# Output projection by seven products in place of eight, in an encoder step of two mixers

## The chip, the cores and the metric

The kernel runs on one core of a Trainium2 chip. The metric is the device time in microseconds (us) of one execution, launch to end; lower is better. TensorE (PE in the rows) multiplies matrices, VectorE (DVE), ScalarE (ACT) and GpSimd (POOL) work element by element, and SyncE (SP) issues nearly all DMAs. Each engine takes its instructions in program order and waits on semaphores.

## The reference, cut to what matters

```python
xn = rms_norm(x, norm_g)                      # x: 512 prompt rows and 32 sample rows, 1024 features
h  = xn @ w_in                                # one projection; its columns feed everything below
oa = sparse_attention(...)                    # top-k keys per query, 8 heads of 64
ob = stick_breaking_attention(...)            # 8 heads of 64
ya = (oa * silu(ua)) @ w_a_out                # 512 -> 1024
yb = (ob * silu(ub)) @ w_b_out                # 512 -> 1024
mixed = sigmoid(ga) * ya + sigmoid(gb) * yb
y  = x + mixed @ w_o                          # 1024 -> 1024, the product that is changed
```

All arrays are float32. The new rows of keys and values are outputs too.

## The kernel before, in words

Prompt and sample tokens lie side by side as 544 columns (`NT`), features on the partitions, in 8 chunks of 128 (`KC`). Most products take two halves of 272 columns (`HALF_NT`), one PSUM bank each. To keep float32 accuracy, each operand is split into a high part (ACT copies it to fp32r) and a low part (DVE subtracts the high part from the raw value), and a product is three matmul passes: high by high, high by low, low by high (`PASSES`).

Weights come in units of 256 columns, 1 MB each (`UNITS`). SP loads them into two raw buffers; ACT writes `whi` (`w_high`, L1051) and DVE `wlo` (`w_low`, L1452).

The changed part is the last 105 us. Its stages, in order:

1. Fast gates (L958). The last five gate features are computed by the seven-product form of a 2 by 2 block product: K in two halves, tokens in two halves. The weight sums t1 to t4 and the quarters b11, b22, b21 stand in a slot (two slots of 7 quarters of 512 columns, each with high and low part). Slot 0 lies where queries and keys were, slot 1 over `whi` and `wlo`. DVE makes the weight sums (L1963 to L1968) and takes products off PSUM with ACT.
2. Mixes (L989). For each of 8 output features d (chunks of 128), branch B's product and branch A's product, 48 matmuls of 272 columns. DVE then multiplies both with the sigmoids (L1996), adds them (L1999), ACT makes the high part (L1432) and DVE the low part (L2001) of the mixed value, and the two make the next-but-one unit's weights (`w_high`, `w_low`). Mix d has its own set of four PSUM banks, used by every other d, and waits for the weights and for d-2's banks.
3. Output projection (L1004). 16 groups (8 features, 2 halves) of 24 matmuls. Each group's result is added to a residual copy of x in `res` (L2009) and stored (L555). `out_group` runs the first three groups up to the last K chunk while the last mixed feature is being finished. `whi`/`wlo` are filled by unit, one ahead.

In the mixing stage POOL does nothing: its program ends with the additions for the last sample rows (L2072). Earlier it multiplies attention weights (L2082) and takes roots (L2094).

Of the kernel before, what the change touches and what calls it, by code (L numbers as in the profile page):

```python
# [8 lines left out]
F32 = mybir.dt.float32  # L9
F32R = mybir.dt.float32r  # L10
# [5 lines left out]
P = 128  # L16
# [178 lines left out]
def direct_index(u):  # L195

    return sum(kind != "fast" for _, kind in UNITS[:u])
# [37 lines left out]
OUT_BANK = [4, 5, 6, 7, 0, 1, 2, 3]  # L235
# [15 lines left out]
SUM_STEPS = (0, 1, 3)  # L251
FAST_BANKS = [{"a": 0, "b": 2, "c": 4}, {"a": 1, "b": 3, "c": 5}]
# [6 lines left out]
def build(nc, x_kw_qi, cache_a_k, cache_a_v, cache_idx_k, cache_b_k, cache_b_v, q_norm_g, k_norm_g,  # L259
# [3 lines left out]
    with ExitStack() as ctx:  # L263
# [16 lines left out]
        xhi = by(KC, sb("xhi", KC * NT, F32R)[:, :])  # L280
        xlo = by(KC, sb("xlo", KC * NT, F32R)[:, :])
# [90 lines left out]
        res = by(KC, sb_at("res", KC * NT, F32, at_q)[:, :])  # L372
# [13 lines left out]
        for n, c, h in (("x11", 0, 0), ("x12", 4, 0), ("s3", 0, 1), ("x22", 4, 1)):  # L386
# [5 lines left out]

        slots_hi = [sb_at(f"slot_hi{k}", SLOT, F32R, at)[:, :] for k, at in enumerate((at_q, at_whi))]
# [11 lines left out]
        const_in, cache_i_in, cache_bk_in, cache_bv_in, cache_ak_in, cache_av_in, res_in = (  # L405
            sem(n) for n in ("const_in", "cache_i_in", "cache_bk_in", "cache_bv_in", "cache_ak_in", "cache_av_in",
                             "res_in"))
# [27 lines left out]
        y_done, y_out = sem("y_done"), sem("y_out")  # L435
# [3 lines left out]
        def wview(buf, uu):  # L439

            return by(2 * EC if UNITS[uu][1] == "mix" else KC, buf[:, uu % 2, 0:unit_cols(uu)])

# [38 lines left out]
        def _(sp):  # L481
            def load_unit(name):
# [6 lines left out]
                sp.dma_start(raw[:, uu % 2, 0:unit_cols(uu)], src).then_inc(raw_ready[uu % 2], 16)  # L489
# [57 lines left out]
            for name, _ in UNITS[U["gate2"]:]:  # L547
                load_unit(name)
                if name == "mix2":
                    sp.wait_ge(f_done, len(PRODUCTS) * len(FAST))  # L550
                    sp.dma_start(res, x_kw_qi.rearrange("c p n -> p c n")[:, :, 1:FIRST_AT]).then_inc(res_in, 16)
            for g in range(2 * KC):
                e, h = divmod(g, 2)
                sp.wait_ge(y_out, g + 1)
                sp.dma_start(y_fm[:, e, halved(h)], res[:, e, halved(h)]).then_inc(st_y, 16)  # L555
# [6 lines left out]
        def _(pe):  # L562
# [409 lines left out]
            def mix(d):  # L972
# [20 lines left out]
                mm.then_inc(mix_done, 1)  # L993
# [4 lines left out]
            def out_group(g, chunks):  # L998

                e, h = divmod(g, 2)  # L1000
                uu = U[f"out{e // 2}"]
                for c in chunks:
                    for a, b in PASSES:
                        mm = pe.matmul(ps[:, OUT_BANK[g % 8], 0:HALF_NT], wview(wpart[b], uu)[:, c, P * (e % 2):P * (e % 2) + P],  # L1004
                                       mpart[a][:, c, halved(h)], start=(c + a + b == 0), stop=(c == KC - 1 and a == 1))
                return mm

            pe.wait_ge(mix_used, D // P - 1)
            pe.wait_ge(m_lo, D // P - 1)
            pe.wait_ge(w_lo, direct_index(U["out0"]) + 1)  # L1010
            for g in range(3):
                out_group(g, range(KC - 1))
            pe.wait_ge(m_lo, D // P)
            for g in range(3):
                out_group(g, [KC - 1]).then_inc(y_done, 1)
            pe.wait_ge(mix_used, D // P)
            for g in range(3, 2 * KC):
                if g % 4 == 0:
                    pe.wait_ge(w_lo, direct_index(U[f"out{g // 4}"]) + 1)
                if g >= 8:  # L1020
                    pe.wait_ge(y_out, g - 7)
                out_group(g, range(KC)).then_inc(y_done, 1)

        @block.scalar
        def _(act):
# [408 lines left out]
            for o in range(2, D // UC):  # L1434
                w_high(f"out{o}")
# [764 lines left out]
```

## Time and profile before

| | us |
|---|---|
| median of 3 runs (524.34 to 526.58) | 525.01 |
| the profiled execution, its own time | 523.65 |
| its span in the trace | 521.9 |
| PE busy in the span | 515.1 (99%) |
| DVE busy | 370.7 (71%) |
| ACT busy | 258.2 (49%) |
| POOL busy | 76.7 (15%) |
| output projection, first to last matmul | 470.7 to 519.3 |

The rows below quote lines of the trace. An instruction line begins with its start and duration in us; a bracket at its end tells how long the engine sat idle before it and what ended that.

### The profile page before, as it was taken

What the parts mean: (1) busy time and instruction counts of PE and PEld (TensorE: products, weight loads), DVE (VectorE), ACT (ScalarE), POOL (GpSimd) and SP (SyncE); (2) the same over time, 40 slices, a digit from 0 to 9 for tenths busy, and PEclk for the clock granted to TensorE, in tenths of its full rate; (3) what the DMA queues carried; (4) which work ended last, traced back from release to release, by engine and by line L of the source; (5) the groups of instructions that cost most, each with busy time, mean ns of one, the idle gap of its engine ahead of it and who ended that gap; (6) DMA issues with size and microseconds to landing.
All of it is one profiled execution on the core that took longest, in us unless ns stands there. A gap on an engine that the chain in (4) does not pass through costs nothing.

```text
span 521.9 us, 10124 instructions
## 1 busy us (share of the span) xinstructions
PE 515.1 (99%) x4188; PEld 485.5 (93%) x4188; DVE 370.7 (71%) x718; ACT 258.2 (49%) x434; POOL 76.7 (15%) x73
## 2 busy tenths in 40 slices
PE   8999999999999999999999999999999999999997
PEld 6889999999998988989998888999999999999997
DVE  5878758899979989478857668563987556665331
ACT  7655764344366566864244665653566532231100
POOL 3506000014034314284000000000000000000000
PEclk9999999999999999999999999999999999999999
DMA  7623305142331322023230016020232172245111
GB/s 274 266 80 123 92 1 167 35 168 82 117 133 28 140 82 82 1 82 122 87 113 4 1 47 212 2 82 1 82 105 98 42 252 80 82 162 189 50 52 46
DMA packets 15359, 50.45 MB, mean 97 GB/s; under 512 B 2288, under 2 KB 6000, under 8 KB 11728
## 3 DMA queue, kind: packets, MB, share of 16 engines
q1 hardware_dynamic: 15168, 49.49, 27.6%
q8 instruction: 33, 0.54, 0.4%
q10 hardware_dynamic: 144, 0.30, 0.2%
q14 instruction: 14, 0.11, 0.1%
HBM read 42.82 MB, written 6.82 MB: 95 GB/s over the span
## 4 chain that ended last, share of the span: by engine, by line
PE 91%; DVE 4%; issue 2%; ACT 2%; DMA 1%; ACTq 0%
PE PS L665 40%; PE PS L1004 9%; PE PS L958 8%; PE PS L989 8%; PE PS L619 4%; PE PS L784 3%; PE PS L765 3%; PE PS L649 3%; PE PS L869 2%; PE PS L741 2%; PE PS L710 2%; PE PS L849 1%; PE PS L690 1%; PE PS L598 1%; PE PS L793 1%
## 5 line engine op out<-in xcount | busy, mean ns | idle before, releaser
L665 PE MATMUL PS<-xhi,whi 128*128 128x272 f32 x320 | 94.6, 296 | 0.0
L665 PE MATMUL PS<-xlo,whi 128*128 128x272 f32 x320 | 92.4, 289 | 0.0
L665 PE MATMUL PS<-xhi,wlo 128*128 128x272 f32 x320 | 92.1, 288 | 0.0
L1452 DVE TENSOR_TENSOR wlo<-raw,whi 128x2048 fp32r<-128x2048 f32 (+1 forms) x31 | 64.5, 2080 | 17.3 <-ACT whi L1051 15.9
L665 PE MATMUL PS<-whi,xhi 128*128 128x256 f32 x256 | 73.4, 287 | 0.8 <-DVE nmx L1844 0.8
L665 PE MATMUL PS<-wlo,xhi 128*128 128x256 f32 x256 | 72.4, 283 | 0.0
L665 PE MATMUL PS<-whi,xlo 128*128 128x256 f32 x256 | 71.9, 281 | 0.0
L665 PEld LDWEIGHTS PS<-xhi,whi 128*128 128x128 f32 x320 | 60.3, 189 | 2.9 <-issue 2.3
L1051 ACT ACTIVATE whi<-raw 128x2048 fp32r<-128x2048 f32 (+1 forms) x31 | 52.1, 1682 | 18.2 <-PE PS L1004 18.2
L665 PEld LDWEIGHTS PS<-xhi,wlo 128*128 128x128 f32 x320 | 60.4, 189 | 0.0
L665 PEld LDWEIGHTS PS<-xlo,whi 128*128 128x128 f32 x320 | 60.2, 188 | 0.0
L665 PEld LDWEIGHTS PS<-whi,xhi 128*128 128x128 f32 x256 | 48.2, 188 | 2.4 <-issue 1.2
L665 PEld LDWEIGHTS PS<-whi,xlo 128*128 128x128 f32 x256 | 48.5, 189 | 0.0
L665 PEld LDWEIGHTS PS<-wlo,xhi 128*128 128x128 f32 x256 | 48.2, 188 | 0.0
L2082 POOL TENSOR_TENSOR wk<-wk 128x766 f32<-128x766 f32 (+2 forms) x13 | 27.8, 2140 | 70.6 <-DVE wk L1741 70.6
L1004 PE MATMUL PS<-xhi,whi 128*128 128x272 f32 x128 | 37.0, 289 | 1.1 <-DVE wlo L1452 1.1
L1004 PE MATMUL PS<-xlo,whi 128*128 128x272 f32 x128 | 37.1, 290 | 0.0
L989 PE MATMUL PS<-olo,whi 128*128 128x272 f32 x128 | 37.0, 289 | 0.0
L1004 PE MATMUL PS<-xhi,wlo 128*128 128x272 f32 x128 | 36.8, 288 | 0.0
L1741 DVE TENSOR_TENSOR_SCAN wk<-wk 128x512 f32<-128x512 f32 (+4 forms) x34 | 25.5, 797 | 12.2 <-ACT wk L1219 12.1
L2009 DVE TENSOR_TENSOR res<-res,PS 128x272 f32<-128x272 f32 x16 | 6.8, 436 | 28.0 <-PE PS L1004 28.0
L1244 ACT ACTIVATE wk<-PS 128x768 f32<-128x768 f32 (+1 forms) x24 | 21.1, 880 | 10.8 <-PE PS L765 10.8
(283 smaller groups left out, 1318.2 us busy)
## 6 DMA issues: line engine op xcount, KB each, us to landing
raw<-in_w_units SPq DMA_DIRECT2D x28, 1024.0 KB, 4.9
raw<-in_w_mixes SPq DMA_DIRECT2D x8, 512.0 KB, 3.4
stage<-in_x_kw_qi SPq DMA_DIRECT2D x7, 564.5 KB, 5.1
res<-in_x_kw_qi SPq DMA_DIRECT2D x1, 2176.0 KB, 8.1
out<-res SPq DMA_DIRECT2D x16, 136.0 KB, 1.7
out<-vals SPq DMA_DIRECT2D x2, 1024.0 KB, 6.2
out<-kT SPq DMA_DIRECT2D x1, 1088.0 KB, 8.7
out<-tm SPq DMA_DIRECT2D x1, 1024.0 KB, 8.0
```

The lines of the kernel that those rows point to most:

```text
L619: mm = pe.matmul(ps[:, t, :], xpart[a][:, c, t0:t0 + n], fpart[b][:, c, KW:FIRST], start=False, stop=(c == KC - 1 and k == 2))
L649: mm = pe.matmul(bank[0:2 * DEC, 0:UC], xst[:, c, :], wview(wpart[b], uu)[:, c, :], start=(c + b == 0), stop=(c + b == KC))
L665: mm = pe.matmul(out, lhsT, rhs, start=(k == 0), stop=(k == 23))
L765: last = pe.transpose(ps[:, 4 + r, o:o + P], pr[:, c:c + P], ident)
L958: mm = pe.matmul(ps[:, banks[b], 0:HALF_NT], weights_of(i, form, w)[:, c, :], (s_hi, s_lo)[a][block_][:, c, :], start=(opens and c + k == ...
L989: mm = pe.matmul(ps[:, MIX_BANK[d] + 2 * br + h, 0:HALF_NT], wview(wpart[b], uu)[:, EC * br + c, :], o_of(a, br, c)[:, halved(h)], start=( ...
L1004: mm = pe.matmul(ps[:, OUT_BANK[g % 8], 0:HALF_NT], wview(wpart[b], uu)[:, c, P * (e % 2):P * (e % 2) + P], mpart[a][:, c, halved(h)], sta ...
L1051: act.activation(whi[:, uu % 2, 0:n], raw[:, uu % 2, 0:n], ACT.Copy).then_inc(w_hi, 1)
L1244: last = act.activation(dst[:, :, 0:n], ps[:, 4:6, 0:n], ACT.Copy)
L1452: dve.tensor_tensor(wlo[:, uu % 2, 0:n], raw[:, uu % 2, 0:n], whi[:, uu % 2, 0:n].bitcast(F32), ALU.subtract).then_inc(w_lo, 1)
L1741: last = dve.tensor_tensor_scan(v, v, v, 1.0, ALU.mult, ALU.min)
L2082: pool.tensor_tensor(v, v, rest[:, t % 2, :, 1:n], ALU.mult).then_inc(a_done, 1)
```

## The change

The output projection gets the seven-product form too: each of four units of 256 output columns is a 2 by 2 block product (K halves, two features; K halves, two token halves). So it needs block sums of the mixed values and of the weights. K is split as chunks 0, 1, 4, 5 and 2, 3, 6, 7 (`K_HALVES`), so that a "pair" k joins one chunk of each half, and the sums s1 to s4 are made pair by pair as the mixed features come: POOL makes those of pairs 0 to 2, DVE those of the last pair. ACT and DVE split them (`sum_high_m`, `sum_low_m`). POOL makes the weight sums of all four units (`out_sums`) and the low parts of the first (`first_low`). The first unit uses slot 0, filled while the mixes run; the second uses slot 1, over `whi` and `wlo`, and so is filled after the last mix; the others follow in turn. The two mix units share one raw buffer, the other serves unit 0. The residuals are loaded in four parts into gate buffers that are used up. Each mix's branch B is multiplied with its gate as soon as it is done, branch A after; the last mix is handled by token halves. Products are added to the residual one by one (`out_added`): 8 for the first unit, 7 for each other.

```diff
+K_HALVES = ((0, 1, 4, 5), (2, 3, 6, 7))
+M_FORMS = ("s1", "s2", "s4", "s3")
+FIRST_OUT = [("p1", "b11", "x11", "a"), ("p2", "b21", "x12", "c"), ("p4", "t4", "x22", "d"), ("p5", "t1", "s1", "b"),
+             ("p6", "t2", "s2", "a"), ("p3", "b22", "s4", "b"), ("p7", "t3", "s3", "a")]
+FIRST_TAKEN = [("p1", 0, 0), ("p2", 0, 0), ("p4", 0, 1), ("p5", 1, 1), ("p6", 1, 0), ("p3", 1, 0), ("p7", 0, 1), ("p7", 1, 1)]
...
 @block.sync
+            load_out(0)
+            for name, _ in UNITS[U["mix2"]:U["out0"]]:
+                load_unit(name)
+            load_res(0)
+            load_res(1)
+            load_out(2)
+            load_out(1)
+            load_res(2)
+            load_res(3)
+            load_out(3)
...
 @block.tensor
+            def out(o):
+                for n, form, block_, b in out_products(o):
...
+                    elif n == "p6":
+                        pe.wait_ge(y_added, taken_last(o, "p1"))
+                    elif n == "p3":
+                        pe.wait_ge(y_added, taken_last(o, "p5"))
+                    elif n == "p7":
+                        pe.wait_ge(y_added, taken_last(o, "p6"))
...
+                    for c in range(KC // 2):
+                        if o == 0:
+                            if n == "p1" and c == 0:
+                                pe.wait_ge(m_lo, D // P - 1)
+                            elif n == "p2" and c == KC // 2 - 1:
+                                pe.wait_ge(m_lo, D // P)
+                            elif n == "p4" and c == KC // 2 - 1:
+                                pe.wait_ge(m_lo, D // P + 1)
+                            elif block_ in M_FORMS:
+                                pe.wait_ge(ms_low, m_form(c, block_))
+                        for k, (a, w) in enumerate(PASSES):
...
 @block.vector
-            for d in range(D // P):
-                dve.wait_ge(mix_done, d + 1)
...
+            for d in range(D // P - 1):
+                dve.wait_ge(mix_done, 3 * d + 1)
...
+                gated(d, 1, None)
+                dve.wait_ge(mix_done, 3 * d + 3)
+                gated(d, 0, None).then_inc(mix_used, 1)
...
                 dve.tensor_tensor(gates[d][:, 0, :], gates[d][:, 0, :], gates[d][:, 1, :], ALU.add).then_inc(mixed, 1)
+                m_low(d, 0, HALF_NT if d in K_HALVES[0] else NT, d + 1)
+                if d + 2 < D // P:
+                    w_low(f"mix{d + 2}")
+                if d in (4, 5):
+                    for form in M_FORMS:
+                        sum_low_m(d - 4, form)
...
+            for h in range(2):
+                dve.wait_ge(mix_done, 3 * d + 2 + h)
+                ins = gated(d, 0, h)
...
+                dve.tensor_tensor(gates[d][:, 0, halved(h)], gates[d][:, 0, halved(h)], gates[d][:, 1, halved(h)],
+                                  ALU.add).then_inc(mixed, 1)
+                if h == 0:
+                    m_low(d, 0, HALF_NT, d + 1)
+            dve.wait_ge(mixed, d + 2)
+            for form in ("s1", "s2", "s4"):
+                sum_m(form)
+            m_low(d, HALF_NT, NT, d + 2)
+            for form in M_FORMS:
+                sum_low_m(2, form)
...
+            sum_low_m(3, "s1")
+            out_added(0, 0)
+            sum_low_m(3, "s2")
+            out_added(0, 1)
+            sum_low_m(3, "s4")
+            sum_low_m(3, "s3")
+            out_added(0, 2)
+            out_low(1, 0)
+            out_added(0, 3)
...
 @block.gpsimd
+            def out_sums(o):
+                pool.wait_ge(out_raw[o % 2], 16 * (o // 2 + 1))
+                if o == 0:
+                    pool.wait_ge(f_done, len(PRODUCTS) * len(FAST))
+                elif o == 1:
+                    pool.wait_ge(mix_done, 3 * D // P)
+                else:
+                    pool.wait_ge(y_done, len(PRODUCTS) * (o - 1))
...
+                pool.tensor_tensor(both, raw_of(uu)[:, QUARTER:3 * QUARTER], raw_of(uu)[:, 0:2 * QUARTER],
+                                   ALU.subtract).then_inc(yt_done, 1)
...
+            out_sums(0)
+            for j in range(len(PARTS)):
+                first_low(j)
+            for k in range(KC // 2 - 1):
+                pair_sums(k)
+            for o in range(1, OUTS):
+                out_sums(o)
```

`out_sums` has one subtraction of 1024 columns and two of 512 that wait for one another; `first_low` four subtractions (512, then three of 1024); `pair_sums` one addition and three subtractions of 272.

## Rows read from the trace of the kernel before

**Rows 1.** The page's busy time: and the granted clock in tenths, 40 slices.
```profile
PE 515.1 (99%) x4188; PEld 485.5 (93%) x4188; DVE 370.7 (71%) x718; ACT 258.2 (49%) x434; POOL 76.7 (15%) x73
...
PEclk9999999999999999999999999999999999999999
```
**Rows 2.** Chain of work that ended last, from 400 us: start, duration, what, count.
```profile
399.97 21.47 PE PS L958 x171
421.44 42.16 PE PS L989 x336
...
466.33 1.91 ACT whi L1051
...
468.26 2.30 DVE wlo L1452
...
470.70 48.58 PE PS L1004 x384
...
519.30 0.44 DVE res L2009
```
**Rows 3.** TensorE's instructions in order of time, where the output projection begins.
```profile
469.20 0.28 PE L989 MATMUL PS<-ohi_a,wlo 128*128 128x272 f32 x1
469.32 0.29 PE L989 MATMUL PS<-olo,whi 128*128 128x272 f32 x1
470.70 0.37 PE L1004 MATMUL PS<-xhi,whi 128*128 128x272 f32 x1 [1.09 <-DVE wlo L1452]
```
**Rows 4.** VectorE's instructions in order of time, around the last two mixes.
```profile
463.62 1.35 DVE L1996 TENSOR_TENSOR gates_v<-gates_v,PS 128x544 f32<-128x544 f32 x2 [1.01 <-PE PS L989]
465.01 0.72 DVE L1999 TENSOR_TENSOR gates_v<-gates_v 128x544 f32<-128x544 f32 x1
466.46 0.73 DVE L2001 TENSOR_TENSOR xlo<-gates_v,xhi 128x544 fp32r<-128x544 f32 x1 [0.72 <-ACT xhi L1432]
```
**Rows 5.** VectorE's groups, shapes apart: count, busy us, mean ns.
```profile
L1926 DVE TENSOR_TENSOR slot_lo<-slot_t,slot_hi 128x1024 fp32r<-128x1024 f32 x10 | 12.1, 1221 | 2.1 <-ACT slot_hi L1381 2.1
L2009 DVE TENSOR_TENSOR res<-res,PS 128x272 f32<-128x272 f32 x16 | 6.8, 436 | 28.0 <-PE PS L1004 28.0
L1926 DVE TENSOR_TENSOR slot_lo<-raw,slot_hi 128x512 fp32r<-128x512 f32 x5 | 3.4, 689 | 5.5 <-ACT slot_hi L1381 5.5
```
**Rows 6.** ScalarE's groups from 340 us, shapes apart.
```profile
L1381 ACT ACTIVATE slot_hi<-slot_t 128x1024 fp32r<-128x1024 f32 x10 | 10.6, 1060 | 2.6 <-DVE slot_t L1879 1.4 <-DVE slot_t L1963 0.7 <-DVE slot_t L1884 0.4
L1399 ACT ACTIVATE gates_v<-PS 128x272 f32<-128x272 f32 x12 | 4.8, 397 | 9.3 <-PE PS L958 9.3
```
**Rows 7.** VectorE in order of time, where several instructions follow without a gap.
```profile
421.01 2.62 DVE L1863 TENSOR_TENSOR olo<-oT,ohi_a 128x544 fp32r<-128x544 f32 x4
479.37 1.13 DVE L2009 TENSOR_TENSOR res<-res,PS 128x272 f32<-128x272 f32 x3 [1.97 <-PE PS L1004]
```
**Rows 8.** POOL in order of time: multiplications beside which no two-input VectorE instruction runs.
```profile
173.05 2.00 POOL L2082 TENSOR_TENSOR wk<-wk 128x1022 f32<-128x1022 f32 x1 [5.02 <-DVE wk L1741]
187.54 1.54 POOL L2082 TENSOR_TENSOR wk<-wk 128x766 f32<-128x766 f32 x1 [4.23 <-DVE wk L1741]
```
**Rows 9.** POOL in order of time: additions.
```profile
46.54 1.28 POOL L2051 TENSOR_TENSOR tm<-tm,oT 32x512 f32<-32x512 f32 x1
215.31 0.73 POOL L2072 TENSOR_TENSOR tm<-tm,bias_r 32x256 f32<-32x256 f32 x1 [3.04 <-ACT bias_r L1143]
```
**Rows 10.** All engines in order of time: POOL and VectorE meet, three places.
```profile
148.41 2.27 DVE L1452 TENSOR_TENSOR wlo<-raw,whi 128x2048 fp32r<-128x2048 f32 x1
148.57 3.96 POOL L2082 TENSOR_TENSOR wk<-wk 128x1022 f32<-128x1022 f32 x1 [17.38 <-DVE wk L1741]
...
221.06 2.00 POOL L2082 TENSOR_TENSOR wk<-wk 128x1022 f32<-128x1022 f32 x1 [5.02 <-DVE wk L1741]
221.23 3.97 DVE L1452 TENSOR_TENSOR wlo<-raw,whi 128x2048 fp32r<-128x2048 f32 x1
...
247.09 1.21 POOL L2082 TENSOR_TENSOR wk<-wk 128x574 f32<-128x574 f32 x1 [5.03 <-DVE wk L1741]
247.26 2.12 DVE L1710 TENSOR_TENSOR tm<-tm,gk 128x1024 f32<-128x1024 f32 x1
```
**Rows 11.** The same view: one-SBUF-input VectorE instructions while POOL works.
```profile
187.39 0.85 DVE L1617 MAX8 top<-bias 128x8 f32<-128x384 f32 x2
...
223.01 5.29 POOL L2094 TENSOR_TENSOR nrs<-nss,halves 128x8 f32<-128x8 f32 x2
...
227.05 0.69 DVE L1749 TENSOR_TENSOR oT<-PS,oT 128x512 f32<-128x512 f32 x1
```
**Rows 12.** The page's DMA issues: KB each, us to landing.
```profile
raw<-in_w_units SPq DMA_DIRECT2D x28, 1024.0 KB, 4.9
```

More of the change, by code:

```diff
@@ L195, in direct_index @@
 def direct_index(u):
-    return sum(kind != "fast" for _, kind in UNITS[:u])
+    return sum(kind not in ("fast", "out") for _, kind in UNITS[:u])
 def fast_index(u):
@@ L371, in build @@
         mhi, mlo = xhi, xlo
-        res = by(KC, sb_at("res", KC * NT, F32, at_q)[:, :])
+        res = [gates[d] for d in (0, 1, 4, 5)]
         half_x = KC // 2 * HALF_NT
@@ L992, in mix @@
                                 k += 1
-                mm.then_inc(mix_done, 1)
+                        if br == 0 or h == 1:
+                            mm.then_inc(mix_done, 1)
             for d in range(D // P):
                 mix(d)
[L998 to L1006, printed above, removed]
@@ L1024, in _ @@
+            for o in range(OUTS):
+                out(o)
         @block.scalar
@@ new lines, in sum_high_m @@
+            def sum_high_m(pair):
+                for form in M_FORMS:
+                    if pair < 3:
+                        act.wait_ge(ms_summed, pair + 1)
+                    else:
+                        act.wait_ge(ms_last, LAST_SUMS[form])
+                    act.activation(m_block(0, form, pair), m_sum(form, pair), ACT.Copy).then_inc(ms_high, 1)
+            for d in range(D // P):
+                if d == D // P - 1:
+                    for h in range(2):
+                        act.wait_ge(mixed, d + 1 + h)
+                        act.activation(mhi[:, d, halved(h)], gates[d][:, 0, halved(h)], ACT.Copy).then_inc(m_hi, 1)
+                        if h == 0:
+                            sum_high_m(2)
+                    sum_high_m(3)
+                    break
+                act.wait_ge(mixed, d + 1)
+                n = HALF_NT if d in K_HALVES[0] else NT
+                act.activation(mhi[:, d, 0:n], gates[d][:, 0, 0:n], ACT.Copy).then_inc(m_hi, 1)
+                if d + 2 < D // P:
+                    w_high(f"mix{d + 2}")
+                if d in (1, 2):
+                    for part in ((0, 3), (1, 2))[d - 1]:
+                        out_high(0, part)
+                elif d in (4, 5):
+                    sum_high_m(d - 4)
@@ L1437, in _ @@
+            for o in range(1, OUTS):
+                for part in (0, 3, 1, 2):
+                    out_high(o, part)
         @block.vector
@@ new lines, in _ @@
+            sum_low_m(3, "s1")
[7 more added lines that the diff above has]
+            out_added(0, 3)
+            out_low(1, 1)
+            out_added(0, 4)
+            out_low(1, 2)
+            out_added(0, 5)
+            out_low(1, 3)
+            out_added(0, 6)
+            out_added(0, 7)
+            for o in range(1, OUTS):
+                out_added(o, 0)
+                out_low(o + 1, 0)
+                out_added(o, 1)
+                out_low(o + 1, 1)
+                out_added(o, 2)
+                out_added(o, 3)
+                out_low(o + 1, 2)
+                out_added(o, 4)
+                out_low(o + 1, 3)
+                out_added(o, 5)
+                out_added(o, 6)
@@ L2159, in laid_out @@
             c = UC * int(name[3:])
-            units.append(by_partition(w_o[:, c:c + UC]))
+            a, b = (by_partition(w_o[:, k:k + P]) for k in (c, c + P))
+            low, high = (list(k) for k in K_HALVES)
+            units.append(np.concatenate([a[:, low], b[:, low], b[:, high], a[:, high]], axis=1).reshape(P, KC, UC))
     def keys(name):
```

267 lines of the change are left out of this document (214 added, 53 removed).

## The prediction

> **What bounds the kernel now.** I read the page's busy times first: TensorE is busy for 515.1 of 521.9 us, so time goes only where TensorE does less or waits [rows 1]. Then the chain of waits from 400 us: it is TensorE nearly throughout, 21.47 us of fast gates, 42.16 us of mixes, and 48.58 us for 384 matmuls of the output projection, 0.1265 us each; the seven-product form runs at the same pace (171 matmuls in 21.47 us, 0.1256) [rows 2]. The only break is where the projection begins: its last predecessor starts at 469.32 and it starts at 470.70, late by 1.25 us, and the bracket names VectorE's low weights [rows 2, 3]. VectorE, ACT and POOL look half idle in shares. What matters is whether they keep up in the stretch around 470 us, for which I laid the changed queues side by side, each in program order, with the durations below.
>
> **What the change removes.** Four units of 7 products of 12 matmuls are 336 in place of 384: 48 × 0.1265 = 6.07 us [rows 2]. The 1.25 us at the start goes, because the first product p1 needs mixed features 0, 1, 4, 5 only and weights that were made during the mixes. Together 7.3 us. The granted clock is full throughout [rows 1]; I take no change.
>
> **What VectorE alone would cost.** Its starts follow each other at 0.65 us for 544 columns (four in 2.62) and 0.35 for 272 (three in 1.13); 0.61 for 512 and 1.14 for 1024 are the durations of rows 5 less the same 0.08 overlap [rows 5, 7]. After the last mix (469.5) it has, before it may take p5: two or three instructions for the last token half, the sums s1, s2, s4, the low part, eight low parts of sums, three `out_added`, and the 512-column low part of unit 1. That is 6 × 0.35 with their waits, then 11 × 0.35 + 0.61, and p5 taken at about 477.4 us. TensorE wants it for p3 after 60 matmuls, at 477.1. So 0.3 us of stall. ACT's part is shorter (272 columns 0.40, 1024 columns 1.06 us [rows 6]) and runs ahead. The three later units ask VectorE for 7 × 0.35 + 0.61 + 3 × 1.14 = 6.5 us in a period of 84 × 0.126 = 10.6, and hide it. With the mixes untouched the gain would be 7.3 − 0.3 = 7.0 us.
>
> **What POOL costs.** It gets 3 instructions for unit 0, 4 low parts, 12 pair sums, and 3 for each other unit; these lie beside VectorE's work. The trace shows two things on them.
>
> First their price. Multiplications take 1.54 us for 766 columns and 2.00 for 1022 [rows 8], so 2.00 for 1024, 1.10 for 512 and 0.68 for 272 by the same line. Additions take 0.73 for 256 and 1.28 for 512 [rows 9], so 2.40 for 1024 and 0.76 for 272 by theirs. The change's instructions are subtractions and additions. I take the additions' line and keep the multiplications' as the lower end. The Trainium skill (GPSIMD Engine Reference, section 3.1) gives 4.5 us for an addition of 2048 columns, by which 1024 would be an estimated 2.25; no row here shows that size.
>
> Second, POOL and VectorE exclude each other when both read two operands from SBUF. A multiplication of 2.00 us begins at 221.06, a VectorE subtraction at 221.23, and the latter takes 3.97 in place of 2.27: it ends 2.1 us after POOL is done. At 247.09 the same: 2.12 in place of 1.2. The other way round, POOL takes 3.96 in place of 2.00 behind a subtraction that began first [rows 10]. Whoever asks second waits for the whole instruction. VectorE instructions with one SBUF operand, or one of two in PSUM, keep their durations [rows 11], so `gated` and `out_added` are exempt; additions of the mixed values, all low parts and sums are not. The Trainium skill (SBUF — State Buffer, section "Who interferes with whom") says that a VectorE instruction with two SBUF inputs contends with a GpSimd one that reads SBUF, and that the second is fully blocked. The trace agrees (3.97 for 2.27). Without that rule the sum would be the 7.0 us of gain above; with it, what follows.
>
> (a) Mix 0. `out_sums(0)` is released with the last fast gate, at 421.45, where VectorE starts four low parts of 0.65 us that mix 0's branch A waits for chunk by chunk (at 424.5, 424.8, 425.2, 425.6) [rows 7]. Alternating, POOL holds 421.5 to 424.0, then VectorE one, POOL 1.28, VectorE one, POOL 1.28, VectorE the last, to 427.9. Chunk 2 comes about 1.1 us late, chunk 3 a further 1.3: 2.4 us, against none now. By the multiplications' line 1.6.
>
> (b) Mixes 2 to 7. From the end of each mix VectorE now needs 0.65 (branch A) + 0.65 (add) + 0.66 of ACT + 0.4 to 0.7 (low part) + 1.14 (low weights) before the next-but-one mix [rows 4, 6], some 4.4 of 6.0 us. Up to three of these wait for a POOL instruction. `first_low` holds 2.4 us at a time in mixes 3 and 4, and the pair sums 0.76 each in mixes 4 and 5, where VectorE also gets the 0.35 us sums. The low weights of mixes 5 and 7 then come 0.5 and 0.3 us late: 0.8 us (0.45 at the lower price).
>
> (c) The end of mix 7. `mix_done` releases VectorE's last token half and `out_sums(1)` at one moment. With time from that moment: POOL holds 0.1 to 2.5; VectorE's add waits and runs to 2.9; POOL to 4.2, s1 to 4.6, POOL to 5.9, s2 to 6.3, s4 6.7, the low part of feature 7's second half 7.1. TensorE wants that for p4's last chunk after 33 matmuls, at 4.15. It stalls 3.0 us, and a further 0.7 because pair 2's sums on POOL (4 × 0.76 after feature 6, itself late) have pushed the first half of feature 7: 3.7 us. By the multiplications' line 2.1. Behind it VectorE runs its list without a pause and is late for p5 by 0.2 and for p3 by 1.2: 1.4 us at either price, the 0.3 above included.
>
> (d) Units 1 to 3. POOL's 5 us and VectorE's 4.0 us of two-operand work make 9.0 of 10.6 us, and fit; one product of unit 1 waits 0.4 us.
>
> SP's queue: unit 0's megabyte goes ahead of mix 2's weights at 410 us and lands within about 5 us [rows 12], before it is asked for at 421; unit 1's is asked for when mix 7's low weights are done, some 5 us before the mixes end, and stands behind nothing that waits. The residual parts replace one load of the same bytes. The tail after the last matmul, one addition and one store, stays. I put these at nothing; if unit 1's load were 1 us later it would cost nothing still, since ACT gets to it only when the sums are done.
>
> **The sum.** −6.07 − 1.25 + 2.4 + 0.8 + 3.7 + 1.4 + 0.4 = +1.4 us by the additions' line; −7.3 + 1.6 + 0.45 + 2.1 + 1.4 = −1.75 by the multiplications'. The profiled execution took 523.65 us of its own, span 521.9, so 525.0 by the first; the median of the runs shown is 525.01, 1.4 above it, and I forecast on that: 526.4 us. Its own range, 523 to 528.
>
> **Rivals.**
> Rival 1, subtraction at the multiplications' price, same exclusion: −1.75, 523.3 us. For it: subtraction could be as fast as multiplication on POOL. Against: the two additions lie on one line well above it [rows 9].
> Rival 2, POOL's holds fall beside VectorE's gaps (VectorE's queued instructions keep the port, POOL waits): only the 0.3 us stall is left, 518.0 us. For it: VectorE's instructions overlap by 0.08 us, and no row shows a burst of two-operand ones against a waiting POOL. Against: in rows 10 the first to ask got it each time. A mixed outcome, (a) gone and half of (c), gives about 522.
> Rival 3, slower: VectorE falls behind in the mixes. The place is the low weights of mixes 5 and 7. Their slack is 1.6 us per mix, and each POOL instruction that is 10% dearer than rows 9 extends (a) to 2.9, (b) to 2.2, (c) with its tail to 5.9 and (d) to 0.9: 11.8 us of stalls, 529.5 us. It decides from 2.6 us for 1024 columns. Each restart of TensorE may add 0.1 (0.37 in place of 0.29 [rows 3]), which works the same way.
> Rival 4, the change doesn't cut the matmuls: the products' list has seven entries of 12, so I give this no chance.
>
> **How the numbers follow.** Forecast 0.45, rival 1 0.2, rival 2 with its mixed form 0.17, rival 3 0.18. A measurement of this kernel can tell about 0.5%, 2.6 us. Faster by more than that (below 522.4): most of rival 2 and a little of rival 1, 0.22. Slower (above 527.6): rival 3 and some of the forecast, 0.28. Within 0.5%: 0.50. The range of 8 in 10 leaves out the pure form of rival 2 and the end of rival 3: 519.5 to 529.5 us.
>
> **What the changed profile would show.** The projection's matmuls number 336, at 0.126 us apart from stalls. TensorE's stalls: in mix 0 branch A on VectorE's low parts (2.4), at the mixes' weights (0.8), in p4 of unit 0 on the low part (3.7), in p3 of unit 0 on VectorE (1.2). VectorE's low parts at 421 us take up to 2.9 us each in place of 0.72, its add after the last mix about 2. POOL's 1024 columns take 2.40 where nothing blocks them, and over 3 where something does. If these VectorE instructions keep 0.72 and 0.43 us beside a busy POOL, the exclusion is not what I take it for and rival 2 holds. If POOL's 1024 takes 2.0, rival 1. Large stalls on DMA, ACT or the fourth unit would show a step that I have not seen.

## The result, and the profile after

The kernel after takes 527.76 us (median of 5 runs, 526.96 to 529.21), the kernel before 524.34 (5 runs, 524.03 to 526.58, among them the three whose median of 525.01 the forecast stood on). The ratio, of the means, is 1.0057, with a 95% interval of 1.0030 to 1.0084: slower by 0.6%, just past the 0.5% that the prediction drew as its line. The profiled execution took 526.96 us, with a span of 525.1, against 523.65 and 521.9.

The page after, which answers to [rows 1]: TensorE does 48 matmuls fewer (4140 for 4188) in a span 3.2 us longer, and one slice has a lower granted clock.

```profile
span 525.1 us, 10182 instructions
PE 512.5 (98%) x4140; PEld 481.6 (92%) x4140; DVE 400.8 (76%) x762; ACT 270.1 (51%) x463; POOL 123.1 (23%) x101
PEclk9999999999999999999999999999999999998999
```

TensorE's instructions in order of time, every place in the last 105 us where it waited (start, duration, and in brackets the idle time and its releaser):

```profile
427.02 0.39 PE L1105 MATMUL PS<-ohi_a,whi 128*128 128x272 f32 x1 [1.07 <-DVE olo L2043]
...
428.73 0.39 PE L1105 MATMUL PS<-ohi_a,whi 128*128 128x272 f32 x1 [1.08 <-DVE olo L2043]
...
455.56 0.39 PE L1105 MATMUL PS<-ohi_b,whi 128*128 128x272 f32 x1 [0.60 <-DVE wlo L1632]
...
468.14 0.39 PE L1105 MATMUL PS<-ohi_b,whi 128*128 128x272 f32 x1 [0.24 <-DVE wlo L1632]
...
482.22 0.60 PE L1153 MATMUL PS<-xhi,slot_hi 128*128 128x272 f32 x1 [3.63 <-DVE xlo L2188]
482.62 0.43 PE L1153 MATMUL PS<-xhi,slot_lo 128*128 128x272 f32 x1
482.84 0.43 PE L1153 MATMUL PS<-xlo,slot_hi 128*128 128x272 f32 x1
...
496.62 0.36 PE L1153 MATMUL PS<-xhi,slot_hi 128*128 128x272 f32 x1 [0.25 <-DVE wk L2254]
```

Read them from start to start: a bracket begins only where the matmul before has ended, 0.29 us after its start, and matmuls that don't wait follow at 0.126; it also leaves out the restart, the slower first matmul behind a wait. The matmul ahead of 427.02 starts at 425.66, 1.36 us earlier and not 0.126: 1.23 lost, and another 0.10 before the next one. So the places cost 2.66 us in mix 0 (two stalls), 0.86 and 0.50 at mixes 5 and 7, 3.78 in p4 of unit 0, and 0.48 in unit 1's p7: 9.8 us with the 1.5 that follow below. The start of the projection, 1.25 us late before [rows 3], is smooth. Every releaser is a VectorE instruction of the kind the prediction named. A further 1.5 us lies behind p4's stall: from 482.22 to 485.50 stand 14 matmuls, the second 0.40 us behind the first and the others at 0.23 us in place of 0.126. The windows show why, in the granted clock (the column behind POOL's):

```profile
476.00:480.00 4.00, 2.60 (x21) 2.37 (x19) 3.90 (x4) 1.54 (x6) 3.84 (x3) 1.00 0.47 141
480.00:484.00 4.00, 1.78 (x8) 1.78 (x9) 3.97 (x9) 2.96 (x7) 1.04 (x1) 0.75 0.25 51
484.00:488.00 4.00, 4.00 (x28) 4.00 (x28) 4.00 (x9) 1.96 (x3) 0.00 (x0) 0.82 0.23 90
```

TensorE lost 3.8 us to this wait, and the matmuls behind it ran at the lower level of the clock, 1.2 GHz, until 485.4; then it was back at 2.4.

VectorE in order of time, at mix 0 and after the last mix, and below it POOL in the same stretches:

```profile
421.68 6.99 DVE L2043 TENSOR_TENSOR olo<-oT,ohi_a 128x544 fp32r<-128x544 f32 x4
...
476.32 2.17 DVE L2232 TENSOR_TENSOR gates_v<-gates_v 128x272 f32<-128x272 f32 x1
478.53 1.39 DVE L2183 TENSOR_TENSOR ms_sum<-gates_v 128x272 f32<-128x272 f32 x1
479.95 1.39 DVE L2183 TENSOR_TENSOR ms_sum<-ms_sum,gates_v 128x272 f32<-128x272 f32 x1
481.37 0.44 DVE L2183 TENSOR_TENSOR ms_sum<-gates_v,ms_sum 128x272 f32<-128x272 f32 x1
481.73 0.43 DVE L2188 TENSOR_TENSOR xlo<-gates_v,xhi 128x272 fp32r<-128x272 f32 x1
```
```profile
422.26 2.40 POOL L2415 TENSOR_TENSOR slot_t<-raw 128x1024 f32<-128x1024 f32 x1 [111.01 <-PE PS L1074]
424.74 1.64 POOL L2418 TENSOR_TENSOR slot_t<-raw,slot_t 128x512 f32<-128x512 f32 x1
426.46 1.64 POOL L2420 TENSOR_TENSOR slot_t<-raw,slot_t 128x512 f32<-128x512 f32 x1
...
475.60 2.60 POOL L2415 TENSOR_TENSOR slot_t<-raw 128x1024 f32<-128x1024 f32 x1
478.28 1.34 POOL L2418 TENSOR_TENSOR slot_t<-raw,slot_t 128x512 f32<-128x512 f32 x1
479.70 1.34 POOL L2420 TENSOR_TENSOR slot_t<-raw,slot_t 128x512 f32<-128x512 f32 x1
```

The four low parts of 421 us took 2.62 before [rows 7] and take 6.99. The addition at 476.32 takes 0.44 where nothing blocks it; it ends at 478.49, behind POOL's 1024 columns, which end at 478.20. The next one waits for POOL's next to end (479.62) and ends at 479.92, and so on: the two engines take turns, one instruction each. The last row, the low part that p4 waits for, is short itself; it is late because of the queue ahead of it.

The balance of the profiled executions: −7.3 us (48 matmuls and the smooth start) + 2.66 + 1.36 + 3.78 + 1.5 + 0.48 = +2.5, against a span longer by 3.2. The other 0.7 is older than the change: by 60 us into the span, in the loads of the start, the execution after is already 0.66 us behind the other (a VectorE instruction starts at 59.98 in the one and at 59.32 in the other). That is no more than two executions of the kernel before differ by: 13 of them on one chip have spans of 521.4 to 522.6.

### The profile page after: what moved, and what is told of

It is laid out like the page before. It is cut to its first block, busy times and chain, and to the rows that moved or that the text cites. A ratio compares the mean times of both kernels' runs of the same rounds, so it can differ in the third digit from the quotient of the medians.

```text
span 525.1 us, 10182 instructions
## 1 busy us (share of the span) xinstructions
PE 512.5 (98%) x4140; PEld 481.6 (92%) x4140; DVE 400.8 (76%) x762; ACT 270.1 (51%) x463; POOL 123.1 (23%) x101
## 4 chain that ended last, share of the span: by engine, by line
PE 84%; DVE 10%; issue 3%; ACT 2%; DMA 1%; ACTq 0%; DVEq 0%
PE PS L781 39%; PE PS L1074 8%; PE PS L1153 7%; PE PS L1105 4%; PE PS L735 4%; PE PS L900 3%; PE PS L881 3%; PE PS L765 3%; PE PS L985 2%; PE PS L857 2%; PE PS L826 2%; DVE olo L2043 1%; DVE wlo L1632 1%; PE PS L965 1%; PE PS L806 1%
## 5 line engine op out<-in xcount | busy, mean ns | idle before, releaser
L781 PE MATMUL PS<-xhi,whi 128*128 128x272 f32 x320 | 94.5, 295 | 0.0
L781 PE MATMUL PS<-xlo,whi 128*128 128x272 f32 x320 | 92.3, 289 | 0.0
L781 PE MATMUL PS<-xhi,wlo 128*128 128x272 f32 x320 | 92.1, 288 | 0.0
L1632 DVE TENSOR_TENSOR wlo<-raw,whi 128x2048 fp32r<-128x2048 f32 (+1 forms) x27 | 55.9, 2069 | 12.9 <-ACT whi L1186 11.5
L1186 ACT ACTIVATE whi<-raw 128x2048 fp32r<-128x2048 f32 (+1 forms) x27 | 44.5, 1649 | 0.6 <-DMA raw<-in_w_units 0.6
L2415 POOL TENSOR_TENSOR slot_t<-raw 128x1024 f32<-128x1024 f32 x4 | 10.3, 2568 | 124.7 <-PE PS L1074 111.0
L1440 ACT ACTIVATE wk<-wk,nmx 128x512 f32<-128x512 f32 (+4 forms) x34 | 18.7, 552 | 14.7 <-DVE nmx L2024 14.7
L1799 DVE MATCH_REPLACE8 bias<-top,bias 128x512 f32<-128x512 f32 (+2 forms) x48 | 25.6, 536 | 0.0
L1797 DVE MAX8 top<-bias 128x8 f32<-128x512 f32 (+2 forms) x48 | 24.4, 540 | 0.0
```

Of the source, the lines that this page charges most:

```text
L781: mm = pe.matmul(out, lhsT, rhs, start=(k == 0), stop=(k == 23))
L1186: act.activation(whi[:, uu % 2, 0:n], raw_of(uu), ACT.Copy).then_inc(w_hi, 1)
L1632: dve.tensor_tensor(wlo[:, uu % 2, 0:n], raw_of(uu), whi[:, uu % 2, 0:n].bitcast(F32), ALU.subtract).then_inc(w_lo, 1)
L1797: ins = dve.max(t8, scores(b))
L1799: ins = dve.match_replace(scores(b), t8, scores(b), TAKEN)
```

## The experiments

In all of them the time is compared with the kernel before on the same chip. The first four share its runs (13, median 523.74), and so do the next four (21, median 523.82).

**All of POOL's new work turned into writes.** The same tiles at the same places, written with a constant, so that sums and low parts are not computed.

```diff
-                pool.tensor_tensor(both, raw_of(uu)[:, QUARTER:3 * QUARTER], raw_of(uu)[:, 0:2 * QUARTER],
-                                   ALU.subtract).then_inc(yt_done, 1)
+                pool.memset(both, 0.5).then_inc(yt_done, 1)
```
(and likewise the other two of `out_sums`, `first_low`, `pair_sums`)

> All new POOL instructions become fills of the same tiles with a constant: same places, same waits, nothing read (the weight sums, the first unit's low parts and the sums of the mixed values are left out of the computation). Theory P (POOL and VectorE exclude each other when both read two SBUF operands): TensorE's stalls of mix 0, of the mixes' weights and of p4 all go, VectorE's add after the last mix takes 0.43 us in place of 2.17, the low parts at 421 us take 0.72; only 0.3 us of stall in p3 of unit 0 is left: 517.4 us, 7 below the kernel before. Rival V (VectorE simply has too much work of its own, or the waits between engines are too long): VectorE's instructions are as many as before, so most of the 9.9 us of stalls stays: above 524.

Measured: 516.76 us (4 runs), ratio 0.9864 (0.9849 to 0.9878), 6.98 us faster than before. VectorE's rows, and POOL's beside them:

```profile
421.06 2.62 DVE L2043 TENSOR_TENSOR olo<-oT,ohi_a 128x544 fp32r<-128x544 f32 x4
...
470.43 0.44 DVE L2232 TENSOR_TENSOR gates_v<-gates_v 128x272 f32<-128x272 f32 x1
```
```profile
421.61 0.96 POOL L2415 MEMSET slot_t<- 128x1024 f32 x1 [110.97 <-PE PS L1074]
...
469.78 0.96 POOL L2415 MEMSET slot_t<- 128x1024 f32 x1 [3.04 <-PE PS L1105]
```

The low parts of 421 us run over the whole of a POOL write (421.61 to 422.57) and take 2.62 as before; the addition at 470.43 begins 0.3 us before the end of another and takes 0.44. All stalls are gone but one of 0.54 us before p3, and the forecast for VectorE alone (a gain of 7.0) is what was measured. This run alone doesn't separate the blocking from POOL's shorter durations (0.96 for 2.40); the rows do for the blocking: 2.62 beside writes and 6.99 beside subtractions.

**POOL's work as multiplications.** `ALU.subtract` and `ALU.add` become `ALU.mult` in all of POOL's new instructions, so that sums and low parts are replaced by products of the same shape.

```diff
-                                   ALU.subtract).then_inc(yt_done, 1)
+                                   ALU.mult).then_inc(yt_done, 1)
```

> All new POOL subtractions and additions become multiplications of the same operands (so the sums and low parts are left out of the computation). Theory P with a price by kind of operation: POOL's 1024 columns take 2.0 us in place of 2.40, 512 take 1.10 in place of 1.34; TensorE's stalls shrink from 9.9 to some 6.5 us: about 524.2 us. If the price goes by columns alone, nothing changes: 527.8. Rival V: nothing changes.

Measured: 527.38 us (4 runs), ratio 1.0061 (1.0044 to 1.0078), as slow as the kernel after. POOL's groups from 400 us, first of the kernel after, then of this one (count, busy, mean ns):

```profile
L2415 POOL TENSOR_TENSOR slot_t<-raw 128x1024 f32<-128x1024 f32 x4 | 10.3, 2568 | 124.7 <-PE PS L1074 111.0 <-PE PS L1153 13.7
```
```profile
L2415 POOL TENSOR_TENSOR slot_t<-raw 128x1024 f32<-128x1024 f32 x4 | 10.2, 2562 | 124.7 <-PE PS L1074 111.0 <-PE PS L1153 13.7
```

The kind of operation doesn't set the price. The prediction took the right price (2.40 unblocked, not 2.00) for a wrong reason; the last two experiments come back to it. This trace also has the lower clock at a place where the other has it not, behind mix 0's second stall of 1.2 us, where 16 matmuls follow at 0.23 us (granted clock in the last but two column):

```profile
428.00:432.00 4.00, 4.00 (x20) 4.00 (x21) 1.02 (x2) 0.00 (x0) 0.00 (x0) 0.57 0.01 4
```

**The first weight sums later.**

```diff
                 if o == 0:
                     pool.wait_ge(f_done, len(PRODUCTS) * len(FAST))
+                    pool.wait_ge(o_lo, 2 * PAIRS)
```

> POOL's weight sums of unit 0 wait for VectorE's last low part of the attention outputs; all else as in the changed kernel. Theory P: the two stalls of mix 0 (2.66 us with their slow restarts) go and nothing comes back, since these sums are needed two mixes later: 525.1 us. Rival V: mix 0's stalls come from VectorE's own queue and stay, 527.8.

Measured: 523.69 us (10 runs), ratio 1.0002 (0.9993 to 1.0012). VectorE and POOL at mix 0:

```profile
421.58 2.62 DVE L2043 TENSOR_TENSOR olo<-oT,ohi_a 128x544 fp32r<-128x544 f32 x4
```
```profile
424.38 2.40 POOL L2416 TENSOR_TENSOR slot_t<-raw 128x1024 f32<-128x1024 f32 x1 [113.22 <-DVE olo L2043]
```

Mix 0 has no stall left, and POOL's three instructions, 2.1 us later (424.38 for 422.26), harm nobody. Relative to before that is 3.5 us better than the kernel after (+3.4 to −0.05), where the stalls and restarts of mix 0 come to 2.66. The other 0.8 is the clock, and not for certain mix 0's. The ten runs here spread too: five at a mean clock of 0.996 or 0.997 take 523.26 to 523.72 us, four at 0.993 take 524.10 to 524.93, one at 1.000 takes 523.47. The trace is of a run at 0.993, with mix 0 undisturbed; behind p4's stall, 3.8 us as in the kernel after, it has 25 slow matmuls where that has 14:

```profile
476.00:480.00 4.00, 0.60 (x2) 0.60 (x3) 3.93 (x7) 1.98 (x6) 2.14 (x2) 0.80 0.00 0
480.00:484.00 4.00, 4.00 (x19) 4.00 (x19) 4.00 (x12) 3.13 (x4) 0.00 (x0) 0.50 0.49 141
```

Compared at 0.997 on both sides (526.96 us, +2.6 to before, and here a median of 523.62, −0.1) mix 0 was worth 2.7, which is what its rows say.

**Unit 1's weight sums on VectorE**, between its additions (`out_added` and `out_low` of unit 1 shift behind them; POOL keeps units 0, 2, 3).

```diff
-            out_low(1, 1)
+            sums_of_1(0)
             out_added(0, 4)
-            out_low(1, 2)
+            sums_of_1(1)
+            out_low(1, 1)
```
(and so on; `sums_of_1` holds the three subtractions of `out_sums(1)`)

> VectorE makes the weight sums of unit 1 itself, spread between the takings of unit 0's products; POOL makes the others. Theory P: p4 of unit 0 no longer waits (3.78 us and the slow clock behind it go), but VectorE now is late for unit 1: by the queues its low parts of t1, t3 come 3.9 us after TensorE wants p5, and p6 waits 1.1 more. So 526 to 528.5 us, hardly better than the changed kernel. A simpler theory (only the moment of the collision is bad) expects the 5.3 us back: 522.5.

Measured: 526.85 us (4 runs), ratio 1.0059 (1.0042 to 1.0076). TensorE's waits (us in all, times, longest), and the place of the longest in VectorE's and POOL's rows:

```profile
PE PS L1154 <- DVE wk L2258: 2.5, 2, 2.0
...
PE PS L1154 <- issue: 0.9, 1, 0.9
```
```profile
488.59 2.71 DVE L2277 TENSOR_TENSOR slot_lo<-slot_t,slot_hi 128x1024 fp32r<-128x1024 f32 x1
```
```profile
486.18 4.05 POOL L2440 TENSOR_TENSOR slot_t<-raw 128x1024 f32<-128x1024 f32 x1 [11.23 <-PE PS L1154]
```

p4's stall is gone (0.17 left), but p3 waits 1.10 us, and unit 1 0.66, 2.14 and 0.63. By starts the places from p4 on cost 5.5 us with their restarts, against 5.8 in the kernel after. Moving the work to VectorE moves the stall: it is now late itself, and its 1024-column low part meets unit 2's sums on POOL.

**p4's gap filled.** 26 matmuls whose result is thrown away go between p2 and p4, about 3.3 us of them, in p4's bank, which p4 starts anew.

```diff
+                    if o == 0 and n == "p4":
+                        for j in range(26):
+                            f = QUARTER * FORMS["b21"]
+                            pe.matmul(ps[:, banks[b], 0:HALF_NT], by(KC // 2, slots_hi[0][:, f:f + QUARTER])[:, j % 4, :],
+                                      m_block(0, "x12", j % 4), start=(j == 0), stop=(j == 25), skip_group_check=True)
```

> The changed kernel with 26 spare matmuls (b21 by x12 high parts, into p4's bank before p4 opens it; their result is dropped) put between p2 and p4 of unit 0, where TensorE otherwise idles for 3.8 us. They need nothing late. In the changed kernel 13 matmuls behind that gap run at a granted clock below 1 (0.23 us apart in place of 0.126), 1.6 us with the slow restart. Theory C (the slow clock behind the gap is a cost of its own): the clock stays at 1, and the time falls by 1.6 us to about 525.5-526. Theory Q (VectorE's queue sets the end of unit 0 anyway): the clock stays at 1 too, but p5 and p3 now wait for VectorE for 0.2 and 1.2 us as the prediction had it, and the time falls by 0.2 us or less: 527-527.5.

Measured: 526.92 us (4 runs), ratio 1.0058 (1.0044 to 1.0072). TensorE's stalls from 476 us:

```profile
482.04 0.39 PE L1158 MATMUL PS<-xhi,slot_hi 128*128 128x272 f32 x1 [0.48 <-DVE xlo L2193]
...
486.90 0.36 PE L1158 MATMUL PS<-s_hi,slot_hi 128*128 128x272 f32 x1 [0.95 <-issue]
```

The granted clock is 1.00 throughout, and nothing is won (+3.1 us to before; the kernel after has +3.4, and +2.6 in its profiled execution): with the clock kept up TensorE comes to p3 at 485.8 and waits 1.1 us for VectorE's queue, the stall that the prediction had there and the kernel after had not. The slow matmuls cost 1.5 us at their place, and 1.4 of it would have been lost at p5 and p3 anyway.

**Only unit 1's weight sums as writes** (unit 1 is computed with constant sums).

```diff
+                if o == 1:
+                    pool.memset(both, 0.5).then_inc(yt_done, 1)
```
(and the same for t2 and t4)

> Only the three POOL instructions for unit 1's weight sums become fills of the same tiles (the sums are left out of the computation); all other POOL work stays. Theory P: the collision after the last mix goes, p4 waits 0.1 to 0.7 us, the clock stays at 1, p3 waits 1.2 us; the stalls of mix 0 and of the mixes' weights stay. 523.5 us, 4 below the changed kernel. Rival: the collision with the pair sums of pair 2 is the main cause of p4's wait, and it stays: 526.5.

Measured: 523.36 us (10 runs), ratio 0.9994 (0.9984 to 1.0004). p4's stall shrinks from 3.78 to 0.17, the lower clock behind it goes, and p3's stall of 1.10 is there; mix 0 and mixes 5 and 7 keep theirs. With restarts the rows say −3.5 at p4, −1.5 of slow matmuls, +0.25 at p5 and +1.2 at p3, so −3.6 against the kernel after; measured, relative to before, −3.9. The clock has a part here too: six of the ten runs are at 1.000 (522.75 to 523.36 us), four at 0.997 (523.96 to 525.30) although p4 no longer stalls. The six have a median of 522.92, −0.9 to before, which is 3.5 better than the profiled execution of the kernel after.

**Only the work during the mixes as writes** (`first_low` and `pair_sums` write constants in place of low parts and sums).

```diff
-                pool.tensor_tensor(slots_lo[0][:, q:q + n], src, slots_hi[0][:, q:q + n].bitcast(F32),
-                                   ALU.subtract).then_inc(y_lo_first, 1)
+                pool.memset(slots_lo[0][:, q:q + n].bitcast(F32), 0.0).then_inc(y_lo_first, 1)
```
(and the four of `pair_sums`)

> The POOL instructions of the mixing stage (the first unit's four low parts and the sums of pairs 0 to 2) become fills; the weight sums of all units stay. Left out of the computation: those low parts and sums. Theory P: the stalls at the weights of mixes 5 and 7 (0.86 and 0.50 us) go, p4's wait falls from 3.8 to 2.6 us, mix 0's stalls stay: 525 us or a little below, 2.2 to 2.6 under the changed kernel.

Measured: 524.32 us (10 runs), ratio 1.0015 (1.0006 to 1.0024). The stalls at mixes 5 and 7 are gone, p4's is smaller:

```profile
479.46 0.39 PE L1153 MATMUL PS<-xhi,slot_hi 128*128 128x272 f32 x1 [2.54 <-DVE xlo L2188]
...
484.31 0.36 PE L1153 MATMUL PS<-s_hi,slot_hi 128*128 128x272 f32 x1 [0.94 <-issue]
```

The ten runs fall into two groups by their mean granted clock: six at 1.000 take 524.04 to 524.46 us, four at 0.993 to 0.997 take 525.36 to 525.54. With p4's stall at 2.7 us the profiled execution kept its clock, and what the four others lost, 1.3 us, was not given back. That is a stretch of lower clock where no later wait absorbs it; behind mix 0's stalls, as the multiplications' trace shows it, is the likely place, since these are left as they were; no trace of such a run was taken. In the kernel after, one run has a mean of 0.997 (the profiled one, 526.96 us), three 0.993 to 0.994 (527.23 to 527.90), one 0.990 (529.21). Which of the two places has the longer stretch of lower clock in those, mix 0 or p4, no trace shows.

**Unit 1 by eight products**, and the first weight sums late. Unit 1 then needs no weight sums at all, at 12 matmuls more; this is the version that the results point to.

```diff
+SECOND_OUT = [("q1", "b11", "x11", "a"), ("q2", "b12", "x11", "b"), ("q3", "b11", "s3", "c"), ("q4", "b12", "s3", "d"),
+               ("q5", "b21", "x12", "a"), ("q6", "b22", "x12", "b"), ("q7", "b21", "x22", "c"), ("q8", "b22", "x22", "d")]
...
-    return PRODUCTS if o else FIRST_OUT
+    return (FIRST_OUT, SECOND_OUT, PRODUCTS, PRODUCTS)[o]
...
+                    pool.wait_ge(o_lo, 2 * PAIRS)
...
+            for o in (2, 3):
+                out_sums(o)
```
(q1, q2 and q5, q6 give the first token half; x11 − s3 is the second half's chunk, so q3 and q4 are subtracted; the weights go in as four quarters, split without sums)

> A version meant to be faster. Unit 0's weight sums wait for the last low part of the attention outputs (as in e3_sums0_late), and unit 1 takes eight products without weight sums: b11 x11 and b12 x11 are taken for the second token half, b11 s3 and b12 s3 are subtracted from it, then the b21 and b22 products follow. Cost: 12 matmuls, 1.5 us. Gain by theory P: POOL's 5 us of unit 1 go from the moment after the last mix (3.8 us of p4's wait with its restart 0.3 and the slow clock 1.3 to 2.5), and VectorE has two low parts of 1024 columns for unit 1 in place of 4.0 us; p3 waits 0.3 us. From e3_sums0_late, equal to the kernel before within 0.1%: 523.7 - 5.9 + 1.5 + 0.3 = 519.6 us, 0.8% below the kernel before. If total VectorE work is what counts, it gains only its 1.7 us less and pays 1.5: 523.5.

Measured: 520.66 us (5 runs, 520.29 to 521.03), ratio 0.9937 (0.9925 to 0.9950): faster than both. TensorE's waits and the addition after the last mix:

```profile
PE PS L1116 <- DVE wlo L1670: 0.8, 2, 0.6
...
PE PS L1182 <- issue: 0.3, 1, 0.3
```
```profile
473.04 0.44 DVE L2270 TENSOR_TENSOR gates_v<-gates_v 128x272 f32<-128x272 f32 x1
```

By starts: −7.3 + 1.5 for the 12 matmuls + 0.86 + 0.51 at mixes 5 and 7 + 0.52 in p4 and p5 + 0.57 at p3 = −3.3; measured −3.2. The expectation was 1.1 lower: it had all of p4's and p5's waits gone, of which 0.52 is left, and 0.3 at p3 in place of 0.57. Against the late sums alone (ratio 1.0002) the eight products are worth 3.1 us.

**POOL's shapes, measured alone.** Ten instructions behind the last addition, where no other engine computes, one waiting for the other.

```diff
+            r0, r1 = raw_of(U["out2"]), raw_of(U["out3"])
+            rows0, rows1 = by(2, r0[:, 0:1024]), by(2, r1[:, 0:1024])
+            link(pool.tensor_tensor(r1[:, 0:1024], r0[:, 0:1024], r0[:, 1024:2048], ALU.subtract))
+            link(pool.tensor_tensor(r1[:, 0:1024], r1[:, 0:1024], r0[:, 0:1024], ALU.subtract))
+            link(pool.tensor_tensor(r1[:, 0:1024], r1[:, 0:1024], r0[:, 0:1024], ALU.mult))
+            link(pool.tensor_tensor(r1[:, 0:1022], r1[:, 0:1022], r0[:, 1:1023], ALU.mult))
+            link(pool.tensor_tensor(rows1[:, :, 0:511], rows1[:, :, 0:511], rows0[:, :, 1:512], ALU.mult))
...
```

> The kernel after with ten POOL instructions appended behind VectorE's last addition, when no other engine computes (its own time is longer by them and says nothing). Open is why the multiplications of before took 2.00 us for 1022 columns where the change's subtractions take 2.40 for 1024. Three differences are left: those were in place, read their second operand one column off, and were two rows of 511. If in place is what is cheap, the subtraction of 1024 columns in place takes about 2.0 against 2.4 into a third place; if the odd offset, the contiguous 1022 with an offset does; if the two rows, the 2 x 511 into another place does too. If none of them, all ten stay on the line of 2.40 per 1024, and the cause is in the data or the tiles. I lean to in place (0.5), rows (0.2), offset (0.1), none (0.2).

POOL's first five rows. The others follow suit: the subtraction of 2 x 511 one column off takes 2.00, the product of 2 x 512 without offset 2.34, that of 2 x 511 one off into another place 1.99, 512 columns 1.26, and 511 one off 1.09.

```profile
523.93 2.34 POOL L2453 TENSOR_TENSOR raw<-raw 128x1024 f32<-128x1024 f32 x1 [15.22 <-DVE gates_v L2254]
526.35 2.34 POOL L2454 TENSOR_TENSOR raw<-raw 128x1024 f32<-128x1024 f32 x1
528.77 2.34 POOL L2455 TENSOR_TENSOR raw<-raw 128x1024 f32<-128x1024 f32 x1
531.18 1.99 POOL L2456 TENSOR_TENSOR raw<-raw 128x1022 f32<-128x1022 f32 x1
533.25 2.00 POOL L2457 TENSOR_TENSOR raw<-raw 128x1022 f32<-128x1022 f32 x1
```

My leaning (in place) was wrong: rows two and three are in place and take 2.34. Offset and count changed together, so one more run.

**Offset and count apart.**

```diff
+            link(pool.tensor_tensor(r1[:, 0:1022], r1[:, 0:1022], r0[:, 0:1022], ALU.subtract))
+            for off in (1, 2, 4, 8, 16, 64):
+                link(pool.tensor_tensor(r1[:, 0:1024], r1[:, 0:1024], r0[:, off:off + 1024], ALU.subtract))
+            link(pool.tensor_tensor(r1[:, 1:1025], r1[:, 1:1025], r0[:, 1:1025], ALU.subtract))
+            link(pool.tensor_tensor(r1[:, 0:1024], r0[:, 1:1025], r0[:, 1024:2048], ALU.subtract))
+            link(pool.tensor_tensor(r1[:, 1:1025], r0[:, 0:1024], r0[:, 1024:2048], ALU.subtract))
```

> The ten probes before this run gave 2.34 us for 1024 columns whatever the operation and the place, and 1.99 for 1022 columns whose second operand lies one column off; the count and the offset changed together. Here a subtraction of 1022 columns without offset, then 1024 columns with the second operand 1, 2, 4, 8, 16 and 64 columns off, both operands and the output one off, only the first operand off, only the output off. If the relative offset of the two operands is what counts, the first takes 2.34, the one-off 2.00, both-off 2.34 again, the first operand alone off 2.00; the steps 2 to 64 show from where it returns to 2.34. If the count (1022) is what counts, the first takes 2.0 and all others 2.34. I lean to the offset (0.8).

POOL's rows for 1022 columns without an offset, then 1024 with the second operand one, two and four columns off, and with both one off:

```profile
523.47 2.34 POOL L2452 TENSOR_TENSOR raw<-raw 128x1022 f32<-128x1022 f32 x1 [15.21 <-DVE gates_v L2254]
...
525.88 2.00 POOL L2454 TENSOR_TENSOR raw<-raw 128x1024 f32<-128x1024 f32 x1
...
527.96 2.00 POOL L2454 TENSOR_TENSOR raw<-raw 128x1024 f32<-128x1024 f32 x1
...
530.04 2.34 POOL L2454 TENSOR_TENSOR raw<-raw 128x1024 f32<-128x1024 f32 x1
...
539.70 2.34 POOL L2455 TENSOR_TENSOR raw<-raw 128x1024 f32<-128x1024 f32 x1
```

The count is not it; the second operand's offset is. One or two columns off, 1024 columns take 2.00 us; 4, 8, 16 or 64 off, or both operands one off, or only the first or only the output off, they take 2.33 to 2.34. The multiplications of [rows 8] had their second operand one column off, the change's subtractions have none.

## Why the prediction was right, and where it was not

The forecast was 526.4 us with a chance of 0.50 for no difference within 0.5%; measured were 527.76 and +0.57%, inside the likeliest case's own range of 523 to 528, on the slower side of the line. The loss itself was forecast at 1.4 us and is 3.4 by the medians. That 526.4 lies only 1.4 short is partly luck: it was counted from 525.01, and the five runs of the kernel before have a median of 524.34, from which the same sum gives 525.7.

- **What it removes, −7.3.** As forecast: 48 matmuls fewer, and no gap at the start of the projection. The run with writes got 6.98 where the forecast for VectorE alone was 7.0.
- **The exclusion.** Shown: VectorE's two-operand instructions take 2.17 for 0.44 beside a subtraction and 0.44 beside a write, and four of them 6.99 for 2.62. The Trainium skill (SBUF — State Buffer, section "Who interferes with whom") says that a VectorE instruction with two SBUF inputs contends with a GpSimd instruction that reads SBUF, and not with one that only writes it; the traces agree. Without this step the forecast would have been about 518. Rival 2 (518 to 522) falls with it.
- **(a) Mix 0, 2.4 forecast, 2.66 at its place**, in the two stalls that it named; the late-sums run removed them. VectorE got in first (421.68, POOL 422.26) and not POOL, which changed nothing in the two stalls. Not forecast: the lower clock behind them, seen in the trace of the multiplications.
- **(b) Low weights of mixes 5 and 7, 0.8 forecast, 1.36.** The places are right (brackets of 0.60 and 0.24 against 0.5 and 0.3); from start to start each costs 0.16 more than its bracket, and 0.1 of restart. The run without POOL's reads in the mixes has neither.
- **(c) p4, 3.7 forecast, 3.78.** The turns came as listed: from POOL's start at 475.60 VectorE's three blocked instructions end after 2.9, 4.3 and 5.7 us, forecast were 2.8, 4.5 and 6.2. But POOL did not start with the end of the mixes: the last mix's last matmul starts at 474.16, and pair 2's sums hold POOL until 475.64. The run with unit 1's sums as writes shows 0.17 there. The 1.4 at p5 and p3 did not appear: 1.5 of slow matmuls took their place, and the filled gap brought the 1.1 at p3 back. That the sum for (c) holds is luck in this part.
- **(d) Unit 1's p7, 0.4 forecast, 0.48.**
- **POOL's price.** The value taken (2.40 for 1024) was right, by the wrong reason; the lower end of the range rested on an offset that the change's instructions don't have. With the right one, rival 1 (0.2) would have been dropped.
- **Rival 3, slower (529.5).** Its mechanism, POOL dearer than 2.6 us, did not come: the unblocked 1024 columns took 2.40. Its side remark on restarts did: 0.1 each, 0.5 in all, charged nowhere in the sum.

The terms came to 8.7 us of new loss against 9.8 in the profiled execution: 0.26 short in (a), 0.56 in (b), 0.18 in (c), 0.08 in (d). About 0.5 of that are restarts. The step that failed is "The granted clock is full throughout; I take no change": it was true of before, but the change puts pauses of 1 to 4 us into TensorE, and the lower clock behind them takes 1.5 us in the profiled execution (where the 1.4 at p5 and p3 went away for it) and about 0.8 more in the median run (527.76 for 526.96). From the right base the account closes: 525.7 + 1.1 for the terms + 0.8 = 527.6. Where the 0.8 lies in the median run is open: the trace of the multiplications has the lower clock behind mix 0, that of the late sums a longer stretch of it behind p4, and the one trace of the kernel after has neither. The 0.7 us of the start is not explained by the change.

## What to carry to other kernels

Before giving work to an idle POOL, list which VectorE instructions beside it read two operands from SBUF, and let the two take turns instruction by instruction: three POOL instructions (2.4, 1.3 and 1.3 us) among short ones that TensorE waits for cost it 2.7 us at mix 0 and most of the 3.8 at p4, and the first three, begun 2.1 us later, cost nothing. Where the algorithm saves TensorE work by sums that other engines make, use it only where these have slack: seven products everywhere lost 0.6%; later sums for the first unit brought that to nothing, and the eight-product form for the one unit whose sums fall at the critical moment then to a gain of 0.6%. A pause that a change adds to TensorE is charged with its restart (0.1 us here), and, as a risk, with a lower clock behind it (1.5 us for 14 matmuls here), unless something behind it is late anyway.

## What the runs showed of the hardware that was not expected

- POOL's two-operand instructions are 15% shorter when the second operand lies one or two float32 columns off the first: 2.00 for 2.34 us at 1024 columns, 1.09 at 511 for 1.26 at 512. Four columns off or more, or the first operand alone off, it is gone. The second operand's own place doesn't decide alone: with all operands and the output one column off it took 2.34. What does decide is open.
- The lower clock came after a pause of 3.8 us, not after 2.7 (profiled execution of the run without reads in the mixes), and yet after two pauses of 1.2 us that were 1.7 us apart, in the trace of the multiplications but not in that of the kernel after. After the same pause of 3.8 us it was granted for 3.4 us in the kernel after (482.0 to 485.4) and for 6.8 us in the run with late sums (478.4 to 485.2).
